# Products of a constant in TensorE's waits between the stages of a two-block transformer kernel

## The reference, cut to what matters

```python
def first_block(x, ...):
    for l in range(DEPTH):                      # 2 layers
        h = rms_norm(x, norm_mix_pre[l])
        proj = h @ w_in[l]
        ...                                     # four branches: two attentions, a convolution, a pooling mixer;
        ...                                     # each is projected up, gated and summed
        x = x + rms_norm(mix, norm_mix_post[l])      # mix = gated sum @ w_o[l]
        f = rms_norm(x, norm_ffn_pre[l])
        ...                                     # up projection, a depthwise convolution of width 3, a gate, down projection
        x = x + rms_norm(f, norm_ffn_post[l])
    return x

def second_block(x, ctx, ...):                  # the part that bears on this change, last layer shown
    hx = x * (1.0 + sc_a) + sh_a
    x = layer_norm_2(alpha * x + g_a * latent_mixer(hx, ctx_side, p, cos, sin), ln1_g[l], ln1_b[l])
    x = layer_norm_2(alpha * x + g_f * hier_moe(x * (1.0 + sc_f) + sh_f, p), ln2_g[l], ln2_b[l])
    return x

def hier_moe(h, p):
    ...                                         # routing: a group and experts inside it, weights `combine`
    gate = jnp.einsum('td,edf->tef', t, p['w_gate'])
    up = jnp.einsum('td,edf->tef', t, p['w_up'])
    hid = jax.nn.silu(gate) * up * combine[..., None]
    return jnp.einsum('tef,efd->td', hid, p['w_down']).reshape(b, L, d)
```

## Time and profile before

| | us |
|---|---|
| three runs | 1764.80, 1766.88, 1767.66 (median 1766.88) |
| profiled execution, its own time | 1761.71 |
| its span in the trace | 1759.8 |
| TensorE busy | 1638.6 (93%) |
| DVE busy | 1145.5 (65%) |
| ScalarE busy | 799.2 (45%) |
| GpSimd busy | 246.7 (14%) |
| mean granted clock of TensorE | 0.959 |

### The profile page before, as it was taken

One profiled execution on the slowest core, in us unless ns is written; L12 is line 12 of the kernel. 1 busy time (PEld: TensorE's weight loads), 2 busy tenths in 40 slices (PEclk: granted clock), 3 DMA queues, 4 the chain that ended last, 5 costly groups with the idle time before them and its releaser, 6 DMA issues. The chain is left out here.

```text
span 1759.8 us, 27106 instructions
## 1 busy us (share of the span) xinstructions
PE 1638.6 (93%) x10920; PEld 1415.3 (80%) x10920; DVE 1145.5 (65%) x1541; ACT 799.2 (45%) x1099; POOL 246.7 (14%) x283
## 2 busy tenths in 40 slices
PE   7999999899998999999899998999898888999996
PEld 5887899799986887899699985776475667999996
DVE  4669998556744659998656743686558664555546
ACT  4454654455534454664445533343126543333341
POOL 0200004135301200003234300101320000000000
PEclk9999999899999999999899999999979987999998
DMA  6454545466554554545366554322100232455552
GB/s 258 173 209 173 192 168 186 150 240 239 182 201 139 190 192 168 193 170 189 132 239 239 191 191 164 135 96 76 45 25 1 72 120 96 168 180 179 191 179 83
DMA packets 40123, 282.10 MB, mean 160 GB/s; under 512 B 4816, under 2 KB 5072, under 8 KB 6864
## 3 DMA queue, kind: packets, MB, share of 16 engines
q1 hardware_dynamic: 38432, 273.15, 42.9%
q10 hardware_dynamic: 1584, 7.43, 1.2%
HBM read 279.51 MB, written 1.05 MB: 159 GB/s over the span
## 5 line engine op out<-in xcount | busy, mean ns | idle before, releaser
L429 DVE TENSOR_TENSOR ring_low<-ring,sb_hi 128x2048 fp32r<-128x2048 f32 x116 | 271.5, 2340 | 183.8 <-ACT sb_hi L424 183.6
L424 ACT ACTIVATE sb_hi<-ring 128x2048 fp32r<-128x2048 f32 x116 | 222.5, 1918 | 280.0 <-DMA ring<-weights 121.4
L578 PE MATMUL psum<-sb_hS,sb_hi 128*128 128x256 f32 x704 | 203.0, 288 | 9.5 <-DVE ring_low L429 9.5
L581 PE MATMUL psum<-sb_hS,sb_hi 128*128 128x256 f32 x704 | 199.6, 284 | 0.0
L582 PE MATMUL psum<-sb_hS,ring_low 128*128 128x256 f32 x704 | 198.9, 283 | 0.0
L840 PE MATMUL psum<-sb_hfT,ring_low 128*128 128x256 f32 x704 | 198.6, 282 | 0.0
L1849 DVE TENSOR_TENSOR sb_split<-ring,sb_split 128x2048 fp32r<-128x2048 f32 x48 | 109.9, 2292 | 94.6 <-ACT sb_split L1844 94.3
L578 PEld LDWEIGHTS psum<-sb_hS,sb_hi 128*128 128x128 f32 x704 | 133.9, 190 | 19.9 <-DVE ring_low L429 12.8
L2248 PE MATMUL psum<-sb_hfS,sb_split 128*128 128x256 f32 x512 | 146.5, 286 | 2.8 <-PE psum L2270 2.1
L2251 PE MATMUL psum<-sb_hfS,sb_split 128*128 128x256 f32 x512 | 146.1, 285 | 0.0
L2252 PE MATMUL psum<-sb_hfS,sb_split 128*128 128x256 f32 x512 | 146.0, 285 | 0.0
(11 more groups left out here) (441 smaller groups left out, 4064.5 us busy)
## 6 DMA issues: line engine op xcount, KB each, us to landing
ring<-weights SPq DMA_DIRECT2D x256, 1024.0 KB, 4.8
sb_rows_ffn<-rows ACTq DMA_DIRECT2D x4, 512.0 KB, 4.4
sb_rows_mix<-rows ACTq DMA_DIRECT2D x2, 1024.0 KB, 7.5
sb_rows<-rows ACTq DMA_DIRECT2D x1, 2048.0 KB, 10.4
sb_x<-x_in SPq DMA_DIRECT2D x2, 512.0 KB, 5.7
sb_y<-ctx_in SPq DMA_DIRECT2D x1, 1024.0 KB, 6.2
out<-sb_x SPq DMA_DIRECT2D x2, 512.0 KB, 2.6
sb_const<-const SPq DMA_DIRECT2D x1, 711.0 KB, 13.3
```

Of the source, the lines that this page charges most:

```text
L424: act.activation(hi_of(n), ring[:, c % SLOTS, :], ACT.Copy).then_inc(hi_ready, 1)
L429: eng.tensor_tensor(low_of(n), ring[:, SPLIT_CHUNKS[n] % SLOTS, :], hi_of(n).bitcast(F32), ALU.subtract).then_inc(lo_dve, 1)
L578: mm = pe.matmul(out, hi[:, k, bs], hS[:, 0, k, :], start=(k == 0), stop=False)
L581: pe.matmul(out, hi[:, k, bs], hS[:, 1, k, :], start=False, stop=False)
```

## The change

A helper `keep_busy(n, name)` claims the bank of job `name` and issues n products of the 128 x 128 identity with itself into that bank's first 128 columns. It signals nothing, and nobody reads what it writes; the job proper starts with products that overwrite the bank. It is called in five kinds of place: ahead of the transposes of the norm before the feed-forward part in both layers (25), ahead of those at the start of layer 1 (31, none in layer 0), behind the last product of layer 1 (13), and in the second block ahead of the transposes of the first tile of rows (8), of the second (11) and ahead of the wait for their draining (7). The order of the experts' chunks is unchanged, as is all else.

```diff
+BUSY_TURN, BUSY_END, BUSY_NORM = (25, 31), 13, (8, 11, 7)
...
+        def keep_busy(n, name):
+
+            jobs.claim(pe, name)
+            for _ in range(n):
+                pe.matmul(jobs.out(name)[:, 0:P], ident, ident, start=True, stop=True)
+
+        def turn_normed(kind, turn, busy=0):
+
+            keep_busy(busy, (kind, 0, 0))
             for t in range(TT):
                 pe.wait_ge((normed_act, normed_dve)[t], turn)
                 for c in range(2):
...
-        turn_normed("ht", 1)
+        turn_normed("ht", 1, BUSY_TURN[1] if l else 0)
...
-        turn_normed("hf", 2)
+        turn_normed("hf", 2, BUSY_TURN[0])
...
         jobs.wait_filled(pe, ("down", 1, 1))
         pe.sem_inc(used[state["owed"]], 1)
+        if l == LAYERS - 1:
+            keep_busy(BUSY_END, ("down", 0, 0))
...
+            def keep_busy(n, name):
+
+                jobs.claim(pe, name)
+                for _ in range(n):
+                    pe.matmul(jobs.out(name)[:, 0:P], ident, ident, start=True, stop=True)
+
+            for t in range(TT):
+                keep_busy(BUSY_NORM[t], ("hf", 0, t))
                 for c in range(2):
                     pe.wait_ge(n_ready, 2 * t + c + 1)
                     transpose4(("hf", c, t), [res[:, t, (4 * c + i) * P:(4 * c + i + 1) * P] for i in range(4)])
+            keep_busy(BUSY_NORM[2], "routeS")
             for t in range(TT):
                 for c in range(2):
                     jobs.wait_drained(pe, ("hf", c, t))
```

More of the change, by code:

```diff
@@ L524, in next_split @@
             return hi_of(n), low_of(n)
-        def turn_normed(kind, turn):
+        def keep_busy(n, name):
[4 more added lines that the diff above has]
+            keep_busy(busy, (kind, 0, 0))
             for t in range(TT):
```

## The result

The changed kernel took 1750.68 us (median of 4 runs, 1744.36 to 1753.32) against 1767.27 of the kernel before: ratio 0.9898, 95% interval 0.9878 to 0.9919, or 16.6 us less. The prediction had 9.5 us less and a range down to 1752.5. Measured again in the experiments it took 1752.47 against 1765.28, ratio 0.9924 (0.9903 to 0.9945), 12.8 us. The median of all ten runs of the changed kernel is 1751.5, and they reach from 1744.36 to 1755.35.

A forecast was written before the change was run, and what follows sets the result against it. TensorE, busy 93% of the span, was taken as the bound nearly everywhere; gains of 3.0 + 1.8 + 3.0 + 0.5 + 1.2 = 9.5 us took 1766.9 to 1757.4 us, range 1752.5 to 1763.5.

The forecast's parts named there:

- What bounds it: Whole kernel: TensorE, busy 93% of the span, is the bound nearly everywhere; standing still and a reduced clock cost time.
- the price: Each added product in the waits: 0.225 us, bounds 0.225 and 0.255; 0.45 at the half clock.
- A: Layer 0, norm before the feed-forward part: 25 products fit the 6.62 us wait, 3.0 us gained.
- B: Start of layer 1: 31 products in a wait of 7.4 us, 1.8 us gained.
- C: Layer 1, norm before the feed-forward part: 25 products, as A, 3.0 us gained.
- No DMA moves: Whole kernel: the added products leave the DMAs where they were; no size given.
- rival 2: TensorE arrives early and waits for split weights; only A and C gain, 6.0 us: 1760.9 us, chance 0.08.
- D: End of the layers, start of the second block: 13 products, +0.5 us taken, bounds -0.5 and +2.8.
- E: Norm before the experts: 8, 11 and 7 products fit their waits, 1.2 us taken between 0 (or -0.5) and 2.5.
- I let it all arrive at the end: Behind each place: TensorE's own work follows and weights shift with it, so all 9.5 us reach the end.
- Rival 1: Clock falls between transposes and next products; only earlier starts count: 3.2 us, 1763.7 us, chance 0.15.
- the page's rule: Transposes don't count as activity, so the clock would fall in A and C, giving Rival 1's sum.

The follow-up runs named there:

- e6: Changed kernel with half the added products at each place (12 and 15; 6; 4, 5, 3): 1763.0 us against 1764.71 of the kernel before, ratio 0.9996.
- e3: Kernel before with added products only at E (8, 11, 7): 1765.72 us against 1765.28, ratio 0.9994.
- e9: Changed kernel with both 128-row edits, those of e7 and e8: 1739.77 us, ratio 0.9859 to the kernel before.
- after: Trace of the changed kernel from its first measurement, set against the kernel before: median 1750.68 us against 1767.27, ratio 0.9898.
- e2: Kernel before with added products only at D (13): 1760.11 us, ratio 0.9973 to the kernel before.
- e4: Changed kernel with each added product replaced by two transposes of the identity: 1746.3 us against 1764.71 of the kernel before, ratio 0.9898.
- e7: Changed kernel with the products spreading the experts' weights contracting over 128 rows instead of 16: 1747.59 us against 1764.87 of the kernel before, ratio 0.9908.
- e12: e9 plus 6 products ahead of D's wait, 13 and 12 in E, 6 behind the routing products: 1737.39 us, ratio 0.9836 to the kernel before.
- e10: Changed kernel plus 8 products behind D's transposes, 13 and 12 in E, 6 behind routing: 1753.44 us against 1764.71 of the kernel before, ratio 0.9945.
- again: Trace of the unaltered changed kernel, measured again in the experiments: 1752.47 us against 1765.28 of the kernel before, ratio 0.9924.
- e1: Kernel before with added products only at A, B and C (25, 31, 25): 1754.91 us, ratio 0.9943 to the kernel before.
- e5: Changed kernel with the added products using 16 of the 128 rows: 1764.25 us, ratio 0.9998 to the kernel before.
- e8: Changed kernel with the second block's scan products that spread the decays contracting over 128 rows instead of 32: 1740.49 us, ratio 0.9862 to the kernel before.

## Why the prediction was wrong

*What bounds it, the price, A, B, C:* right (but for slice 40 of the clock's line, which stands at 8 too). A product cost 0.223 to 0.229 us by the distance of starts (A's 50 MATMULs take 5.75 us with the last one's tail). A gave 3.3 us for 3.0: the start of the next stage came 1.1 us sooner (338.41 - 327.08 = 11.33 against 336.10 - 325.84 = 10.26, from the start of the last product ahead) where I had 0.7, and the cold products 2.2 where I had 2.3. C the same, B 1.7 for 1.8. The last product ahead of A in the kernel before:

```profile
327.08 0.39 PE L818 MATMUL psum<-sb_hi,sb_mixS 128*128 128x512 f32 x1
```

*"No DMA moves":* wrong in one place. Behind A one chunk's low part came 0.76 us late (line 844 at 425.01), and that stretch lost 0.6 to 0.8 us in all ten traces with 25 products in A. This looks like rival 2, but TensorE's early arrival isn't the reason: the rows of 16, where A gained 0.1 us, lost 0.6 too. The chunk itself came late. From issue to landing it took 7.9 to 8.2 us in these ten traces and 6.6 to 6.8 in the four others. In the ten, a 16 KB packet of the queue that the profile calls "instruction" falls 5.1 to 5.4 us behind the chunk's issue; in e6 it falls 6.1 us behind it, in the other three after the chunk has landed. That the packet delays the chunk isn't shown, only that the two go together. ScalarE's wait for the chunk and the chunk's time to landing, each before and after:

```profile
423.74 1.92 ACT L424 ACTIVATE sb_hi<-ring 128x2048 fp32r<-128x2048 f32 x1 [5.90 <-DMA ring<-weights]
420.71 1.92 ACT L425 ACTIVATE sb_hi<-ring 128x2048 fp32r<-128x2048 f32 x1 [8.27 <-DMA ring<-weights]
...
ring<-weights SPq DMA_DIRECT2D x1, 1024.0 KB, 6.7
ring<-weights SPq DMA_DIRECT2D x1, 1024.0 KB, 8.2
```

*D and E:* the first failed step, as a size. "I take +0.5" and "I take 1.2" were guesses between bounds of -0.5 to 2.8 and 0 to 2.5. In the seven traces with D's 13 products (or the 26 transposes in their place) and its pauses open, the clock held throughout in five (2.5 us each), in one in part (1.7) and in one not at all. In seven with 8, 11, 7 in E it held in five (2.3 us each), not in e3, and only partly in e9 (0.9). That gives 2.0 and 1.8 us on the mean, 2.1 us more together than I took. The start of E's products gained nothing where I had 0.2.

*"I let it all arrive at the end":* the second failed step, and the larger. I took every other stretch as unchanged, because what follows each place "is TensorE's own work" and shifts with it. It doesn't shift unchanged, since the clock falls at other points of it. Three stretches gained:

- Behind D, 1.6 us on the mean of the seven traces. In the kernel before the clock falls at 1152 us. That fall stayed away, and 1.8 to 2.0 us were gained, in six of the seven traces in which D held throughout (after, e2, e4, e7, e9, e12); it came in the seventh (e10). It came where D fell in again, e1, e3 and e5, and stayed away in e6, where D fell, and in e8, where D fell in part. So the two mostly go together, but each is seen without the other.
- At the spreading of the experts' weights, 1.9 to 2.1 us in the five traces in which E held and this stretch is as in the change (after, again, e4, e8, e10), 0.0 to 0.1 in the four in which E gained nothing. Over the five traces that have the 8, 11 and 7 products and this stretch as in the change (after, again, e3, e4, e8) the mean is 1.6.
- In layer 1's mixer, 1.6 us on the mean where A, B and C held, as said under e1.

Why the falls come and go together isn't shown. Nor is it clear that the gain behind D lasts. From there to the end of the scan the four traces with D held and the scan as in the change (after, e2, e4, e7) lost 1.3 us on the mean against the kernel before, the five with D fallen (again, e1, e3, e5, e6) 2.3, and single traces lie between 1.1 gained and 5.6 lost.

*The sum:* A to E and the gains behind D and E come to 3.3 - 0.8 + 1.8 + 3.3 + 2.0 + 1.6 + 1.8 + 1.6 = 14.6 us on the mean, with the mixer 16.2. The two measurements gave 16.6 and 12.8. What is left is no more than what untouched stretches do: the scan's row of the table ranges over 7 us, and in no trace with the scan's products as they were was it noticeably shorter than in the profiled execution of the kernel before. The distance of 16.6 from 12.8 us I leave unexplained, as scatter of the runs.

*The range:* its lower end was the sum of all upper bounds, 13.6 us, and 0.8 us for the spread of the runs. The ten runs of the changed kernel spread over 11 us. The first median lay 1.8 us below the range. The second, 1752.47, lay at its lower end, though its gain of 12.8 us is inside the sum's bound; beside it the kernel before took 1765.28, not 1766.9.

*Rival 1 and the page's rule:* the Trainium skill, "TensorE: Matmul & The Clock Gate", Part 4, has transposes not counted as activity. The page's own times there are of bf16 transposes; these are f32. e4's trace disagrees: with transposes alone A ran at 1.00 and the kernel was 18.4 us faster. The rule shouldn't have had a part in rival 1's 0.15. Short pauses, its other ground, are found where the outcome varied, in D and E, twice in succession (1.94 and 1.91 us; 1.42 and 1.63 us with narrow products between); in A and C (0.93 and 1.24 us) the clock held in all nine traces with full products or transposes. With D's second pause filled it held in both traces (e10, e12), which is too few to show that the pauses decide.

## What to carry to other kernels

A wait of TensorE cost twice here: its own length, and, in A and C, the next stage's transposes and first 5 us of products at half clock. Products that nobody reads, cut to the measured wait at their price in a stream, took back the second part; half as many took back nothing. Look for stretches of low clock where TensorE is busy as well: where the products there use few rows, giving them all 128 helped twice here, and in the scan it took off another 8 to 12 us on the medians. Where pauses of 1.4 to 2 us followed each other the outcome varied between traces, so count such a place with a mean of several traces, not with one. And don't take the stretches behind as unchanged: align the traces product by product and see.

## What the runs showed that I had not expected

- Transposes held the clock as products do (e4), and products over 16 of 128 rows didn't, with TensorE as busy (e5). In e7 the same products ran at 0.97 with 128 rows, after 0.60 with 16; only their operand's place in memory changed besides.
- A fall of the clock at 1074 us mostly goes with another some 80 us later, at 1152 us, worth 1.9 us; of 14 traces, three (e6, e10 and, with half a fall in D, e8) had one without the other.
- 25 added products in A went with a chunk of weights some 85 us further on that took 1.4 us longer to land, in ten traces of ten.
- The same kernel's scan took 92.9 or 100.2 us in two executions, at a mean clock of 0.82 or 0.74.
